# Recurrent block of a two-block network kernel: where the next weights are split, and decays and scans over tile pairs

## What is computed

```python
def rglru_mixer(h, w_in, conv_w, conv_b, w_a, b_a, w_x, b_x, lam, w_out):
    B, S, _ = h.shape
    gate, u = jnp.split(h @ w_in, 2, axis=-1)
    u = lax.conv_general_dilated(u, conv_w[:, None, :].astype(u.dtype), window_strides=(1,),
                                 padding=[(CONV_WIDTH - 1, 0)],
                                 dimension_numbers=('NWC', 'WIO', 'NWC'),
                                 feature_group_count=RNN_WIDTH) + conv_b
    ub = u.reshape(B, S, RNN_BLOCKS, RNN_BLOCK_W)
    r = jax.nn.sigmoid(jnp.einsum('bsnd,nde->bsne', ub, w_a) + b_a).reshape(B, S, RNN_WIDTH)
    i_g = jax.nn.sigmoid(jnp.einsum('bsnd,nde->bsne', ub, w_x) + b_x).reshape(B, S, RNN_WIDTH)
    log_a = -RG_C * jax.nn.softplus(-lam.astype(jnp.float32)) * r.astype(jnp.float32)
    a = jnp.exp(log_a)
    b = jnp.sqrt(-jnp.expm1(2.0 * log_a)) * (i_g * u).astype(jnp.float32)
    _, hs = lax.associative_scan(lin_rec, (a, b), axis=1)
    y = hs.astype(h.dtype) * jax.nn.gelu(gate)
    return y @ w_out

# second layer of second_block
mix = rglru_mixer(hh, ...)
x = x + g1 * mix
hh = rms_norm_2(x, norm2_g[layer]) * (1.0 + sc2) + sh2
x = x + g2 * swiglu(hh, ffn_w_in[layer], ffn_w_out[layer])
```

## Time and profile before

| what | value |
|---|---|
| device time, median of 3 runs | 1705.2 us (1703.02 to 1705.38) |
| span of the profiled execution | 1698.1 us |
| what the runs' median holds beyond that span | 7.1 us |
| TensorE matmuls busy | 1445.4 us, 85% of the span |
| TensorE weight loads busy | 1122.2 us, 66% |
| VectorE busy | 813.1 us, 48% |
| ScalarE busy | 591.3 us, 35% |
| chain that ended last: TensorE's share | 29% |

### The profile page before, as it was taken

One profiled execution on the slowest core, in us unless ns is written; L12 is line 12 of the kernel. 1 busy time (PEld: TensorE's weight loads), 2 busy tenths in 40 slices (PEclk: granted clock), 3 DMA queues, 4 the chain that ended last, 5 costly groups with the idle time before them and its releaser, 6 DMA issues. The chain is left out here.

```text
span 1698.1 us, 26707 instructions
## 1 busy us (share of the span) xinstructions
PE 1445.4 (85%) x11126; PEld 1122.2 (66%) x11126; DVE 813.1 (48%) x1371; ACT 591.3 (35%) x849; POOL 21.9 (1%) x34
## 2 busy tenths in 40 slices
PE   5999998999966666566656599989999999799999
PEld 3889886678842221121211487559999998799999
DVE  4353426766541101001010578656776466977753
ACT  3432135774321001010000352745343456754331
POOL 1100000000000000000000000000000000100000
PEclk8999999999969777786776799999999999899999
DMA  9765357642759999999999754854555444345520
GB/s 395 309 229 199 149 214 275 252 169 108 285 197 393 429 427 428 427 427 429 427 428 427 326 224 177 344 199 171 177 184 189 174 174 149 125 174 183 190 100 25
DMA packets 48990, 437.68 MB, mean 258 GB/s; under 512 B 5232, under 2 KB 7664, under 8 KB 8304
## 3 DMA queue, kind: packets, MB, share of 16 engines
q1 hardware_dynamic: 47872, 430.99, 64.4%
q10 hardware_dynamic: 1008, 5.07, 0.7%
HBM read 434.99 MB, written 1.05 MB: 257 GB/s over the span
## 5 line engine op out<-in xcount | busy, mean ns | idle before, releaser
L771 PE MATMUL bank<-arena_r,ring_r 128*128 128x256 f32 (+1 forms) x5016 | 703.6, 285 | 22.1 <-DVE ring_r L1844 8.9
L771 PEld LDWEIGHTS bank<-arena_r,ring_r 128*128 128x128 f32 x5016 | 654.8, 191 | 38.4 <-issue 26.3
L1844 DVE TENSOR_TENSOR ring_r<-ring,ring_r 128x2048 fp32r<-128x2048 f32 x108 | 247.2, 2291 | 175.0 <-ACT ring_r L1493 174.7
L1140 PE MATMUL bank<-ring,arena 128*32 128x512 f32 x1008 | 168.4, 804 | 120.2 <-DMA ring<-in_w 117.9
L1493 ACT ACTIVATE ring_r<-ring 128x2048 fp32r<-128x2048 f32 x108 | 205.7, 1906 | 128.2 <-PE bank L771 119.1
L1140 PEld LDWEIGHTS bank<-ring,arena 128*32 128x32 f32 x1008 | 33.8, 129 | 243.1 <-DMA ring<-in_w 141.1
L771 PE MATMUL bank<-H_r,ring_r 128*128 128x256 f32 x816 | 182.6, 289 | 4.7 <-DVE H_r L1821 4.6
L771 PEld LDWEIGHTS bank<-H_r,ring_r 128*128 128x128 f32 x816 | 137.2, 196 | 8.1 <-issue 7.4
L2111 DVE TENSOR_TENSOR arena<-arena,bank 64x512 f32<-64x512 f32 x16 | 11.1, 692 | 273.2 <-ACT arena L1603 273.2
L1603 ACT ACTIVATE arena<-bank 64x512 f32<-64x512 f32 x16 | 9.4, 588 | 357.7 <-PE bank L1140 357.7
L771 PE MATMUL bank<-arena_r,ring_end_r 128*128 128x256 f32 (+1 forms) x400 | 114.5, 286 | 0.0
(11 more groups left out here) (283 smaller groups left out, 1482.7 us busy)
## 6 DMA issues: line engine op xcount, KB each, us to landing
ring<-in_w SPq DMA_DIRECT2D x93, 2048.0 KB, 25.7
ring<-in_w SPq DMA_DIRECT2D x171, 1024.0 KB, 5.0
ring_end<-in_w SPq DMA_DIRECT2D x45, 1024.0 KB, 4.9
ring<-in_bias ACTq DMA_DIRECT2D x1, 2048.0 KB, 12.3
ring_end<-in_w SPq DMA_DIRECT2D x1, 2048.0 KB, 23.6
H<-in_w SPq DMA_DIRECT2D x2, 1024.0 KB, 12.5
consts<-in_consts ACTq DMA_DIRECT2D x1, 1183.0 KB, 9.4
X<-in_x SPq DMA_DIRECT2D x1, 1024.0 KB, 5.5
```

Of the source, the lines that this page charges most:

```text
L771: i = nc.tensor.matmul(o, lhsT, rhs, start=start, stop=stop, skip_group_check=grouped)
L1140: last = matmul(bank[0][32 * j:32 * j + 32, :], x_cur[:, k, :], columns(slot_of(c), j, 512), start=k == 0, stop=k == KT - 1)
L1844: v.tensor_tensor(r(lo), lo, r(hi), ALU.subtract).then_inc(lo_ready, 1)
```

## The change

It does four things, all in the recurrent block.

1. **Input tiles.** For a split that stands in front of an `rnn_in` step, the lo half moves behind that step: on VectorE, `scale_tile` and `convolve` of the tile come first and the subtraction after them. ScalarE's order stays.
2. **Output chunks.** Three splits get places of their own (`RNN_SPLITS`). `rnn_out(2)`: hi before the gates, lo before the first `rnn_decay`. `rnn_out(3)`: hi in front of `rnn_gate(8)`, lo in front of the scan of tiles 6 and 7. `rnn_out(4)`: both in front of the scan of tiles 8 and 9. The split of `rnn_out(5)`, whose chunk is half empty, is done on the full half alone.
3. **Pairs.** VectorE's part of the decay and the whole scan step (ScalarE's square root too) run over two tiles at once, 512 columns; tile 10 stays alone. The scan of a pair runs through both tiles; a zero is written into the first column of the second tile's decay (a `memset`), so that nothing is carried over. `rnn_ready` counts pairs.
4. **Order.** `rnn_out(0)` stands after all the scans in the list. As TensorE has no part in decays and scans, its own order is the same.

```diff
@@ plan_steps
     for g, tiles in enumerate(RNN_GROUPS):
         s += [("rnn_gate", i) for i in tiles] + [("rnn_decay", g)]
-
-        s += [("rnn_out", 0)] if g == len(RNN_GROUPS) - 1 else []
-        s.append(("rnn_scan", g))
-    s += [("rnn_out", j) for j in range(1, (RNN_T + 1) // 2)]
+        s += [("rnn_scan", i // 2) for i in tiles[::2]]
+    s += [("rnn_out", j) for j in range((RNN_T + 1) // 2)]
@@ with_splits
+RNN_SPLITS = {("rnn_out", 2): (("rnn_gate", 0), ("rnn_decay", 0)), ("rnn_out", 3): (("rnn_gate", 8), ("rnn_scan", 3)),
+              ("rnn_out", 4): (("rnn_scan", 4), ("rnn_scan", 4))}
+HALF_CHUNK = ("rnn_out", RNN_T // 2)
...
+        x, low = RNN_SPLITS.get(u, (x, x))
         before.setdefault(x, []).append(("split", u))
-        if u in AFTER_LIFT.values():
+        if low != x:
+            before.setdefault(low, []).append(("split_lo", u))
+        elif x[0] == "rnn_in":
+            after.setdefault(x, []).append(("split_lo", u))
+        elif u in AFTER_LIFT.values():
@@ TensorE
             def step_rnn_out(j):
-                pe.wait_ge(rnn_ready, min(2 * j + 2, RNN_T))
+                pe.wait_ge(rnn_ready, j + 1)
@@ ScalarE
+            def step_rnn_scan(p):
+                act.wait_ge(rnn_sqrt_in, p + 1)
+                f(pair_cols(thr, p), pair_cols(thr, p), ACT.Sqrt).then_inc(rnn_sqrt, 1)
@@ VectorE
             def step_rnn_decay(g):
+                for p in range(RNN_GROUPS[g][0] // 2, RNN_GROUPS[g][-1] // 2 + 1):
+                    tiles = rnn_pair(p)
+                    dve.wait_ge(rnn_tanh, tiles[-1] + 1)
+                    d = rnn_d[:, 2 * (p % 2):2 * (p % 2) + len(tiles), :].rearrange("p a b -> p (a b)")
+                    link(v.tensor_tensor(d, pair_cols(rec, p), pair_cols(rec, p), ALU.mult))
+                    v.scalar_tensor_tensor(pair_cols(thr, p), d, 1.0, pair_cols(thr, p), ALU.add,
                                            ALU.mult).then_inc(rnn_sqrt_in, 1)
+            def step_rnn_scan(p):
+                tiles = rnn_pair(p)
+                h, gate = pair_cols(u_c, p), pair_cols(gelu_g, p)
+                if len(tiles) == 2:
+
+                    v.memset(rec[:, tiles[1], 0:1], 0.0).then_inc(dve_step, 1)
+                    steps[0] += 1
+                dve.wait_ge(rnn_sqrt, p + 1)
+                dve.wait_ge(rnn_gated, tiles[-1] + 1)
+                link(v.tensor_tensor(pair_cols(inp, p), pair_cols(inp, p), pair_cols(thr, p), ALU.mult))
+
+                dve.wait_ge(job_done, JOBS[("rnn_gate", min(tiles[-1] + 1, RNN_T - 1))].no)
+                link(v.tensor_tensor_scan(h, pair_cols(rec, p), pair_cols(inp, p), 0.0, ALU.mult, ALU.add))
+                link(v.tensor_tensor(h, gate, h, ALU.mult))
+                link(v.tensor_copy(r(gate), h))
+                v.tensor_tensor(r(h), h, r(gate), ALU.subtract).then_inc(rnn_ready, 1)
```

More of the change, by code:

```diff
@@ L276 @@
 AFTER_LIFT = {name + (0,): name + (1,) for name in FIRST_TILES.values()}
+RNN_SPLITS = {("rnn_out", 2): (("rnn_gate", 0), ("rnn_decay", 0)), ("rnn_out", 3): (("rnn_gate", 8), ("rnn_scan", 3)),
+              ("rnn_out", 4): (("rnn_scan", 4), ("rnn_scan", 4))}
+HALF_CHUNK = ("rnn_out", RNN_T // 2)
 def with_splits(steps):
-    place, before, uses = {}, {}, [x for x in steps if x[0] in SPLIT_STEPS]
+    place, before, after, uses = {}, {}, {}, [x for x in steps if x[0] in SPLIT_STEPS]
     for u in uses:
@@ L301, in with_splits @@
             before[x].append(("split_lo", u))
-    return [y for x in steps for y in before.get(x, []) + [x]], place
+    return [y for x in steps for y in before.get(x, []) + [x] + after.get(x, [])], place
 STEPS, SPLIT_PLACE = with_splits(plan_steps())
@@ L556, in build @@
         rec, inp = room(8481, RNN_T, T), room(11297, RNN_T, T)
-        thr, rnn_d = room(2816, RNN_T, T), room(14113, 2, T)
+        thr, rnn_d = room(2816, RNN_T, T), room(14113, 4, T)
         bank = [ctx.enter_context(nc.psum_tensor(f"bank{i}", [P, 512], F32)) for i in range(8)]
@@ L633, in split_slots, with rnn_pair, pair_cols @@
         def split_slots(key):
-            return place(SPLIT_PLACE[key][0]), place(slot_of(CHUNK_NO[key]))
+            n = CHUNK // 2 if key == HALF_CHUNK else CHUNK
+            return place(SPLIT_PLACE[key][0])[:, 0:n], place(slot_of(CHUNK_NO[key]))[:, 0:n]
+        def rnn_pair(p):
+            return range(2 * p, min(2 * p + 2, RNN_T))
+        def pair_cols(x, p):
+            return x[:, 2 * p:min(2 * p + 2, RNN_T), :].rearrange("p a b -> p (a b)")
         def shift_of(ni, k):
@@ L813, in split_chunk @@
                 pe.wait_ge(lo_ready, SPLIT_NO[key] + 1)
-                return [x.rearrange("p (k n) -> p k n", k=n) for x in split_slots(key)]
+                return [x.rearrange("p (k n) -> p k n", n=CHUNK // n) for x in split_slots(key)]
             def mm3(o, a, b, start, stop, ends=None, grouped=False):
@@ L2299, in step_rnn_decay @@
             def step_rnn_decay(g):
[L2301 to L2304, removed]
-                                           ALU.mult).then_inc(rnn_sqrt_in, 1)
[L2307 to L2314, removed]
-                    link(v.tensor_tensor_scan(u_c[:, i, :], rec[:, i, :], inp[:, i, :], 0.0, ALU.mult, ALU.add))
-                    link(v.tensor_tensor(u_c[:, i, :], gelu_g[:, i, :], u_c[:, i, :], ALU.mult))
-                    link(v.tensor_copy(r(gelu_g[:, i, :]), u_c[:, i, :]))
-                    v.tensor_tensor(r(u_c[:, i, :]), u_c[:, i, :], r(gelu_g[:, i, :]), ALU.subtract).then_inc(rnn_ready, 1)
+                for p in range(RNN_GROUPS[g][0] // 2, RNN_GROUPS[g][-1] // 2 + 1):
[4 more added lines that the diff above has]
+                    v.scalar_tensor_tensor(pair_cols(thr, p), d, 1.0, pair_cols(thr, p), ALU.add,
+                                           ALU.mult).then_inc(rnn_sqrt_in, 1)
```

4 lines of the change are left out of this document (removed).

## The result

The changed kernel takes **1684.49 us**, the median of 4 runs (1684.10 to 1686.03). The kernel before took 1704.11 us, the median of 4 runs (1701.92 to 1705.38), three of which are the ones that the prediction started from. The ratio on record is 0.9899, with a 95% interval of 0.9884 to 0.9914: faster, by some 17 us.

A forecast was written before the change was run, and what follows sets the result against it. TensorE's work plus its waits was taken to bound the recurrent block. Gains of 2.8 + 1.8 + 7.9 + 2.2 + 1.0 less 0.3 made 15.4 us, taken off 1705.2: 1689.8 us, range 1687.0 to 1693.5.

The forecast's parts named there:

- the sum: Recurrent block, all gains and the loss together: 2.8 + 1.8 + 7.9 + 2.2 + 1.0 - 0.3 = 15.4 us.
- Input tiles: Tiles before the gates: with the lo half behind the bank's emptying, one every 5.80 us; 2.8 us gained, at most 3.2.
- Pause in the gates: Before the third gate: its bank is emptied ahead of the lo half, so TensorE's wait goes; 1.8 us gained.
- Output chunks: Waits of 7.9 and 1.0 us and a slow third chunk (2.2 us) go; a new wait gives back 0.3 us.
- The circle: From the end of `rnn_out(0)` through ScalarE and VectorE to `rnn_out(4)`: 18.0 us against 17.7 covered, 0.3 us lost.
- all 7.9 us: TensorE's wait before `rnn_out(2)`: gone once its lo half stands ahead of the first decays; 7.9 us gained.
- 1.6 us of the circle: The two scans between `rnn_out(0)` and `rnn_out(4)`: without pairs they would cost 1.6 us more.
- The extra hi half before the sigmoids: ScalarE, 1.9 us for `rnn_out(2)`: covered, since the sigmoids wait for TensorE's gates anyway; priced at nothing.
- the circle late: Rival, chance 0.17: ScalarE and VectorE are late for `rnn_out(4)`, TensorE waits some 3 us; 1692.5 us.
- without gain at the tiles: Rival, chance 0.07: the lo half is late for its own input tile, so TensorE still waits; 1692.6 us.

The follow-up runs named there:

- the repetition: Each kernel timed and profiled again unmodified: the kernel before against itself, ratio 0.9999; the changed kernel against the kernel before, 1683.79 us, ratio 0.9903.
- the full dose: Changed kernel plus one unused ScalarE square over 2048 columns behind the hi half of `rnn_out(3)`; block 121.70 us, ratio 0.9921 against the kernel before.

## Why the prediction was right and wrong

**The step that failed** is the one with the least thought in it, the base from which the gain was taken off: "The runs' median lies 7.1 us above the span, which I keep: 1705.2 - 15.4 = 1689.8 us." That took a difference between executions, three long ones and a shorter one, for something that stays. The runs show a time 1.8 us above its own span and the kernel before at 1700.8 to 1701.8 us (medians of 11 to 21 runs), so the base was 3.4 to 4.4 us too high; with the 0.8 us that the sum lacked this makes up the miss of 5.3 to within the scatter. Why those three runs were long stays open. The range had the same fault: it allowed "the runs' own spread of some 2 us" downward, where single executions spread over 8 us in the 21 runs. On the profile's own footing the same sum gives 1698.1 + 1.8 - 15.4 = 1684.5 us, but that it hits the measured time is luck: this base was 0.9 to 1.9 us low, the gain 0.8 us short, and the two errors work against each other. The profile of the repetition, an execution of 1706.03 us, would have given 1690.6. Rivals and mechanism had little part in the miss.

**Input tiles:** 2.8 us forecast. From the first of the nine to the first gate it was 1426.80 - 1371.83 = 54.97 us and is 1425.93 - 1374.21 = 51.72: 3.25 us, at the upper bound of that term (3.2), since a tile takes 5.75 us and not 5.80. No wait on the bank is left, and VectorE idles 1.22 us per tile (1.1 forecast).

**Pause in the gates:** 1.8 forecast, 2.1 measured: from first gate to first chunk 1455.78 - 1426.80 = 28.98 us, now 26.87. The idle time in a row counts from the modelled end of the last matmul, and where nothing waits that end lies behind the next start: 1439.77 + 13.38 = 1453.15 in the changed kernel, with the output chunks starting at 1452.80. So a removed wait can give some 0.3 us more than its idle time.

**Output chunks:** 7.9 + 2.2 + 1.0 - 0.3 = 10.8 us forecast. Measured 1500.03 - 1455.78 = 44.25 against 1486.20 - 1452.80 = 33.40: 10.85 us.

**The circle** was right step by step. In the changed kernel ScalarE's and VectorE's timelines read:

```profile
1459.02 1.92 ACT L1510 ACTIVATE ring_r<-ring 128x2048 fp32r<-128x2048 f32 x1 [3.29 <-PE bank L788]
1460.96 1.28 ACT L1712 ACT_TABLE_LOAD   x1
...
1465.76 1.28 ACT L1728 ACT_TABLE_LOAD   x1
1467.06 1.31 ACT L1728 ACTIVATE arena<-arena,sp 128x256 f32<-128x256 f32 x3
...
1471.49 0.94 ACT L1732 ACTIVATE arena<-arena 128x512 f32<-128x512 f32 x2
```

```profile
1460.97 2.29 DVE L1860 TENSOR_TENSOR ring_r<-ring,ring_r 128x2048 fp32r<-128x2048 f32 x1 [2.12 <-ACT ring_r L1510]
1463.19 1.27 DVE L2334 TENSOR_TENSOR arena<-arena 128x512 f32<-128x512 f32 x1
...
1464.49 1.65 DVE L2337 TENSOR_TENSOR_SCAN arena<-arena 128x512 f32<-128x512 f32 x1
...
1468.33 0.69 DVE L2321 TENSOR_TENSOR arena<-arena 128x512 f32<-128x512 f32 x1
...
1470.45 2.28 DVE L1860 TENSOR_TENSOR ring_r<-ring,ring_r 128x2048 fp32r<-128x2048 f32 x1
1472.66 0.69 DVE L2334 TENSOR_TENSOR arena<-arena 128x512 f32<-128x512 f32 x1
...
1473.39 1.23 DVE L2337 TENSOR_TENSOR_SCAN arena<-arena 128x512 f32<-128x512 f32 x1
...
1476.45 0.42 DVE L2334 TENSOR_TENSOR arena<-arena 128x256 f32<-128x256 f32 x1
```

With the end of `rnn_out(0)` put 0.4 us ahead of the hi half, at 1458.6, the lo half begins at 2.4 (2.3 forecast), the decays at 9.7 (9.6), the second lo half at 11.85 (11.8), its scan at 14.1 (14.1), and TensorE's chunk at 1476.59, 18.0 (18.0). The pair took 1476.45 - 1472.66 = 3.8 us as I had chosen between 2.3 and 4.6, with a scan of 1.23 us ("about 1.2"). The wait was 0.82 us, and 0.50 in the repetition, instead of 0.3, because TensorE's row ended a little earlier than after 3 x 5.9 us, not because the circle was longer.

**Where the account was too narrow.** The text gave all 7.9 us to the new places, and to the pairs 1.6 us of the circle. The runs show that pairs alone shorten the block by 4.8 us, with that same wait down from 7.88 to 3.83, and that without them the change loses 4.1. Nor do its terms stand by themselves: with the tiles alone the faster third chunk only lengthened the next wait. And the extra hi half before the sigmoids, put at nothing, costs 1.2 us as soon as the input tiles are late. **The rivals:** the circle late (1692.5 us) and without gain at the tiles (1692.6) did not happen, and the full dose shows how close the first was: 1.9 us more on ScalarE cost 3.0. The rule of the Trainium skill named there (ScalarE: Activation LUTs, "What ACT_TABLE_LOAD costs"), a drain of some 1380 ns with each table load, is not in these rows either: the load at 1465.76 takes 1.28 us and the exps start 0.02 us after it.

## What to carry to other kernels

Before a gain is taken off a time, find out how far that time scatters: neither three runs nor one profiled execution is a base good to 2 us for a kernel whose executions spread over 8, and the range must hold that spread. A gain good to 0.8 us was spoilt by such a base. When a wait ends with one engine's in-order queue, list everything that the queue holds from its last idle moment on: shortening any of it (pairs) and taking the awaited step out of its tail (new places) gain in the same wait, and each alone already gives about half of what they give together (4.8 and 5.4 of 9.6 us). A step priced at nothing because an engine waits there anyway loses its cover when the neighbouring part is undone, and a lengthened wait can cost more than its length where it also brings the clock down (here 3.0 us for 1.5).

## What the runs showed of the hardware

- The clock after idle time: behind waits of 0.82, 1.19, 1.70 (tiles alone) and 1.79 us (the gates before) TensorE was granted 1.00 throughout; behind 2.36, 3.19, 3.83 and 7.88 us it ran for 2 us or more at 0.50 (behind the first, 1476 to 1478 us was still granted 0.97, and 1478 to 1480 us 0.50), which lengthened the chunks behind the first two by 1.5 and 1.3 us and the chunk behind the last by 2.2. These are waits of this block only; what decides between them was not isolated.
- VectorE beside GpSimd's products: a product of 512 columns went from 0.69 us to between 1.03 and 1.27, and its scan from 1.23 to 1.65, an operation of 256 columns from 0.42 to 0.95 or, in the same trace, from 0.43 to 0.77 or 0.84. The excess per operation is 0.3 to 0.6 us at either length. The pair of tiles 6 and 7 took 1468.33 - 1463.19 = 5.1 us, 1.3 more than the free pair, where a tile beside GpSimd took 1.2 more. What the prediction drew from the Trainium skill's page on SBUF (SBUF — State Buffer, "Who interferes with whom"), that longer instructions could lengthen the overlap, hardly showed on VectorE. GpSimd itself went from 3.62 to 4.70 us for its four products beside pairs. But its three products of the third group took 3.50 us beside a pair and 3.45 beside single tiles (the version without pairs), so the length of VectorE's operations is not the only thing that decides there.
- A scan took 0.69 us at 256 columns and 1.23 at 512, while a product of the same tiles took 0.42 and 0.69: the second 256 columns cost the scan 0.54 us and the product 0.27.
